# Stick-breaking attention: the causal mask moved from a product on TensorE into the scan on VectorE

## The reference

```
def sb_attend(q, k, v, q_pos, k_pos):
    z = jnp.einsum('bqhd,bkhd->bhqk', q, k) * SB_DIM ** -0.5
    mask = k_pos[None, :] < q_pos[:, None]
    log_1mb = jnp.where(mask, jax.nn.log_sigmoid(-z), 0.0)
    after = lax.cumsum(log_1mb, axis=3, reverse=True) - log_1mb
    att = jnp.where(mask, jnp.exp(jax.nn.log_sigmoid(z) + after), 0.0)
    return jnp.einsum('bhqk,bkhd->bqhd', att, v)
```

## Time and profile before

| what | value |
|---|---|
| median of 3 runs | 1905.25 us (1903.93 to 1905.9) |
| profiled execution | 1906.05 us |
| its span | 1904.5 us |
| TensorE busy | 1778.7 us, 93% |
| VectorE busy | 1054.4 us, 55% |
| ScalarE busy | 866.0 us, 45% |
| GpSimd busy | 121.9 us, 6% |
| the 68 scans, mean | 1423 ns |

### The profile page before, as it was taken

The page is one execution under the profiler, slowest core; times in us unless marked ns, Lnnn a source line. Parts: engine busy times, 40 slices in busy tenths (PEclk is TensorE's granted clock), DMA queues, the critical chain, the costliest instruction groups (busy, mean ns, idle before and its releaser), DMA issues. The chain is left out here.

```text
span 1904.5 us, 25559 instructions
## 1 busy us (share of the span) xinstructions
PE 1778.7 (93%) x10344; PEld 1564.6 (82%) x10344; DVE 1054.4 (55%) x1291; ACT 866.0 (45%) x1112; POOL 121.9 (6%) x136
## 2 busy tenths in 40 slices
PE   7999999899999999999999999969999999999960
PEld 5887777788898879999999998848888888888850
DVE  4326555333245432133243155568888889889857
ACT  4224554323263331121122223247878878878832
POOL 0013000000000021000000000000010000010003
PEclk9999999899999999999999999979999999999985
DMA  5231110202012226111112142169999999999947
GB/s 177 84 103 39 29 29 1 58 23 71 23 42 78 73 60 209 39 45 51 42 42 94 29 172 89 50 248 367 418 415 416 412 415 415 412 413 418 406 149 271
DMA packets 139179, 329.86 MB, mean 173 GB/s; under 512 B 13659, under 2 KB 91319, under 8 KB 114358
## 3 DMA queue, kind: packets, MB, share of 16 engines
q1 hardware_dynamic: 123556, 272.69, 38.7%
q0 software_dynamic: 10896, 38.74, 5.6%
q10 hardware_dynamic: 4608, 16.78, 2.2%
HBM read 286.08 MB, written 39.87 MB: 171 GB/s over the span
## 5 line engine op out<-in xcount | busy, mean ns | idle before, releaser
L2362 DVE TENSOR_TENSOR low<-raw,hig 128x2048 fp32r<-128x2048 f32 x192 | 431.6, 2285 | 68.2 <-ACT hig L2131 67.6
L2131 ACT ACTIVATE hig<-raw 128x2048 fp32r<-128x2048 f32 x192 | 359.4, 1915 | 23.1 <-ACT ye L2202 14.5
L1984 PE MATMUL bank<-hig,xel 128*128 128x512 f32 x512 | 204.3, 399 | 3.9 <-DVE xel L2429 3.9
L1986 PE MATMUL bank<-hig,xeh 128*128 128x512 f32 x512 | 201.1, 393 | 0.0
L1985 PE MATMUL bank<-low,xeh 128*128 128x512 f32 x512 | 200.8, 392 | 0.0
L71 PE MATMUL bank<-xhi,glo 128*128 128x384 f32 (+1 forms) x552 | 180.1, 326 | 3.6 <-ACT sg L2084 2.2
L73 PE MATMUL bank<-xhi,ghi 128*128 128x384 f32 (+1 forms) x552 | 180.0, 326 | 0.0
L72 PE MATMUL bank<-xlo,ghi 128*128 128x384 f32 (+1 forms) x552 | 179.9, 326 | 0.0
L71 PE MATMUL gproj<-xhi,glo 128*128 128x384 f32 (+1 forms) x408 | 142.4, 349 | 3.0 <-DVE glo L1350 3.0
L72 PE MATMUL gproj<-xlo,ghi 128*128 128x384 f32 (+1 forms) x408 | 137.3, 337 | 0.0
L73 PE MATMUL gproj<-xhi,ghi 128*128 128x384 f32 (+1 forms) x408 | 137.0, 336 | 0.0
(11 more groups left out here) (408 smaller groups left out, 3505.6 us busy)
## 6 DMA issues: line engine op xcount, KB each, us to landing
raw<-in_w_e_gate_dram SPq DMA_DIRECT2D x64, 1024.0 KB, 7.8
raw<-in_w_e_up_dram SPq DMA_DIRECT2D x64, 1024.0 KB, 8.2
raw<-in_w_e_down_dram SPq DMA_DIRECT2D x64, 1024.0 KB, 7.5
graw<-in_w_in_dram SPq DMA_DIRECT2D x40, 512.0 KB, 3.8
expert_rows<-ye ACTq DMA_DIRECT2D x32, 512.0 KB, 8.0
xt<-in_x_prompt_dram SPq DMA_DIRECT2D x16, 512.0 KB, 3.7
expert_rows<-nil POOLq DMA_DIRECT2D x16, 512.0 KB, 10.3
braw<-in_w_branch_dram SPq DMA_DIRECT2D x24, 256.0 KB, 2.8
```

Of the source, the lines that this page charges most:

```text
L1984: nc.tensor.matmul(bank[:, :], xel[n % 2][:, kk, :], wh[:, k, :], start=(kk == 0), stop=False)
L1986: last = nc.tensor.matmul(bank[:, :], xeh[n % 2][:, kk, :], wh[:, k, :], start=False, stop=(kk == KC - 1))
L2131: nc.scalar.activation(hig[q % HI][:, :], raw[q % RAW][:, :], ACT.Copy).then_inc(high, 1)
L2362: nc.vector.tensor_tensor(low[q % RAW][:, :], raw[q % RAW][:, :], hig[q % HI][:, :].bitcast(F32), ALU.subtract).then_inc(lowed, 1)
```

## The change

The 64 mask products of the rounds 0 to 7 are gone, and with them the tile `never` and the VectorE instruction that made it. The last score product of each head signals `scored` itself. The "d" rounds keep their mask and their scan. For the others the scan takes a second input, a bf16 table `over` of 960 columns of 0 followed by 128 columns with 1 where the key is hidden, cut to the round's length and read from the right like `sfx`, and its second operation is a maximum. Since running products are at most 1, a 1 in the table holds the product at 1, and a 0 leaves it as it is. GpSimd builds the table ahead of the first cache difference, VectorE waits for it once, before the first scan of round t = 1, and `attT` moves by 1 KB to make room.

```
-    attT = [at("attT", [P, 512], F32, SUF0 + 9216 + 2048 * i) for i in range(3)]
-    assert SUF0 + 15360 <= END
+    attT = [at("attT", [P, 512], F32, SUF0 + 10240 + 2048 * i) for i in range(3)]
+    over = at("over", [P, T - DEC], BF16, SUF0 + 8192)
+    assert SUF0 + 16384 <= R2 + 49152
...
-    never = at("never", [P, P], BF16, CON + 2560)
...
             nc.gpsimd.memset(cvsh[0:1, 0, :], 0.0)
             pool.drain()
+            nc.gpsimd.memset(over[:, 0:T - DEC - P], 0.0)
+            pool.drain()
+            nc.gpsimd.affine_select(out=over[:, T - DEC - P:T - DEC], in_=ones[:, :], compare_op=ALU.is_ge, fill=0.0,
+                                    base=0, pattern=[[1, P]], channel_multiplier=-1)
+            pool.drain()
+            pool.sem_inc(overlaid, 1)
             cache_differ(0)
...
-                            nc.tensor.matmul(zz[u][:, o:o + w], q, k, start=(i == 0), stop=(i == 2 and not diag),
-                                             skip_group_check=True)
+                            product = nc.tensor.matmul(zz[u][:, o:o + w], q, k, start=(i == 0),
+                                                       stop=(i == 2 and not (end and x == "d")), skip_group_check=True)
+                            if x != "d" and end and i == 2:
+                                product.then_inc(scored, 1)
                     k0 += w
-                o, w = sp2[-1]
-                d0 = o + w - (DEC if x == "d" else P)
-                for u in range(len(unit[t])):
-                    nc.tensor.matmul(zz[u][:, d0:o + w], identb[:, :], neverd[:, :] if x == "d" else never[:, :],
+                if x == "d":
+                    o, w = sp2[-1]
+                    nc.tensor.matmul(zz[0][:, o + w - DEC:o + w], identb[:, :], neverd[:, :],
                                      start=False, stop=True, skip_group_check=True).then_inc(scored, 1)
...
-                nc.vector.tensor_tensor_scan(v, v, v, 1.0, ALU.mult, ALU.bypass).then_inc(scanned, 1)
+                if rounds[owner[n]][1] == "d":
+                    nc.vector.tensor_tensor_scan(v, v, v, 1.0, ALU.mult, ALU.bypass).then_inc(scanned, 1)
+                else:
+                    if owner[n] == 1:
+                        ve.wait_ge(overlaid, 1)
+                    cover = over[:, T - DEC - keys[n]:T - DEC][:, ::-1]
+                    nc.vector.tensor_tensor_scan(v, v, cover, 1.0, ALU.mult, ALU.max).then_inc(scanned, 1)
...
-            nc.vector.tensor_scalar(never[:, :], below[:, :], -1.0, 1e30, ALU.add, ALU.mult)
```

More of the change, by code:

```diff
@@ L214, in build @@
             ctx, "q", "wq_in ck_in cv_in qwh qwl qprod ckturned pahigh palow glrd qbuilt")
-        scored, sdone, scanned, tfilled, tcopied, used, ocopied = sems(
-            ctx, "sb", "scored sdone scanned tfilled tcopied used ocopied")
+        scored, sdone, scanned, tfilled, tcopied, used, ocopied, overlaid = sems(
+            ctx, "sb", "scored sdone scanned tfilled tcopied used ocopied overlaid")
         early_in, late_in, last_in, vcol_in, vdiffed, cvdiffed = sems(
@@ L413, in score @@
                 for c, (o, w) in enumerate(sp2):
-                    diag = c == len(sp2) - 1
+                    end = c == len(sp2) - 1
                     for i in range(3):
```

## The result

| | before | changed |
|---|---|---|
| median, first measurement (6 and 6 runs) | 1904.94 us | 1895.34 us |
| ratio, 95% interval | | 0.994, 0.9926 to 0.9955 |
| median, measured again (17 and 6 runs) | 1907.10 us | 1896.38 us |
| ratio, 95% interval | | 0.9949, 0.993 to 0.9968 |
| span of the profiled execution | 1904.5 us | 1897.0 us, the second time 1892.5 us |

The change saves 9.6 us, in the second measurement 10.7; forecast were 6.4 us, 1898.9, in a range from 1895.8. The single times of the changed kernel lie from 1891.7 to 1903.0 us, those of the kernel before in the second measurement from 1903.6 to 1911.5; the three times shown ahead of the prediction had differed by only 2 us.

A forecast was written before the change was run, and what follows sets the result against it. TensorE was taken to bound the masked rounds. 6.5 us from products, less 0.2 for ScalarE, plus 0.1 for the first rounds, gave 6.4 us saved: 1898.9 us from the median of 1905.25, range 1895.8 to 1902.3.

The forecast's parts named there:

- TensorE is the bound in the rounds: Masked rounds, three and a half of four head pairs: TensorE busy 46.69 of 47.6 us, its time saved shortens the span.
- 0.216 us a round, one change of shape instead of two: Average directly after scores in TensorE's queue: one 0.1 us shape change remains; 30 rounds save 6.5 us.
- costs two: Rival: the direct change from scores to average costs two shape changes; 0.11 us a round, 3.3 us saved, 1902.0; 10%.
- is free: Rival: the direct change from scores to average costs nothing; 9.3 us or so saved, 1896; 6%.
- The contrast in the earlier trace: After four transposes, a same-shape query product follows 0.41 us later, scores of another shape 0.61 (0.59 where nothing waits).
- ScalarE gives 0.06 us back in three rounds: Step from 384 to 640 keys, three head pairs: scores wait for sigmoids, gaining 0.15 instead of 0.22; 0.2 us given back.
- The first rounds, 0.1 us: Rounds t=1 and t=2: scans of 1024 begin 0.15 us earlier, at half clock worth 0.07 to 0.15; 0.1 us gained.
- The scan and the table cost nothing: VectorE's scan with bf16 input and maximum keeps its time; GpSimd builds the table while idle for 5.13 us; 0.
- The rival that ends on the other side: Rival: bf16 stream or true maximum slows the scan; if doubled, 32 us more in all, about 1931; 4%.
- What is won here moves all the rest forward.: Everything after this stage starts behind a barrier, loads too, so the stage's gain moves all later work forward.
- TensorE's clock dips at idle places in later stages can fall differently: Uncertainty in later stages, with three shown runs differing by 2 us: forecast's own range 1897.3 to 1900.7, at 75%.
- The low end of the range, 1895.8: Lower limit of the range holding 8 in 10, which takes in the bounds of the shape change's cost.

## Why the prediction was wrong in size, step by step

- **TensorE is the bound in the rounds.** Right. The head pair came down to 45.90 us, forecast 45.9.
- **0.216 us a round, one change of shape instead of two.** Right: 0.27 us from scores to average, and the kernel with masks of the same shape shows the price of a change by itself. The rivals "costs two" and "is free" fall. The contrast in the earlier trace rows was read too smoothly: 0.41 against 0.59 us is 0.18, not 0.1. Taken over all products of the three full-clock head pairs, a change costs 0.10 to 0.15 us, and the larger figure stands at changes from and to the transposes, which are in both kernels.
- **ScalarE gives 0.06 us back in three rounds.** Right, 0.05.
- **The first rounds, 0.1 us.** Not confirmed. The term rested on one trace. What the first head pair takes varies by 2.3 us in kernels with mask products and by 1.5 us in those without, mostly with the clock. Where TensorE was at 1.2 GHz for 6.8 us of it, it took 51.9 and 52.6 us with mask products and 51.0 and 50.8 without; where for 10.2 us, 54.3 and 53.9 against 52.4 and 52.2. That is a gain of 1.4 us and of 1.8, near the 1.4 that the terms make, but so few traces do not resolve 0.1.
- **The scan and the table cost nothing.** Right, taken together (1906.61 against 1907.10), and the scan by itself: 2280 ns as before. The rival that ends on the other side falls.
- **"What is won here moves all the rest forward."** This is the step that failed. It put what the later stages gain at nothing, and they did not just start earlier: they took 3.1 us less in the mean of four traces, by 6.8 us less time at 1.2 GHz. I had allowed under 2 us either way (1897.3 to 1900.7) for "TensorE's clock dips at idle places in later stages can fall differently", and took the narrow spread of the three times shown for the size of that effect. It is larger: adding 2.6 us of idle time to the kernel before takes 3.7 us off, adding 64 short products to the changed one adds 4.4, of which 1.5 lie in the attention stage. The low end of the range, 1895.8, came from the change of shape alone and left it no room. Why the clock is low for less time there stays open.

What the change does in its own stage is therefore the 6.4 us of the forecast (6.6 in the rounds of the traces). The remaining 3 to 4 us of its gain come from the clock in stages that it does not touch, and another edit may take them back, as the 64 products took some 3 us.

## What to carry to other kernels

Count changes of TensorE's array shape as well as products: a small product whose shape differs from its neighbours' on both sides costs its own time and one change more, here half of its price. A mask that keeps a running product at 1 cost nothing here as the scan's second operation. And where a program has stages in which TensorE idles now and then, a gain of a few microseconds upstream is known only to within the clock's answer downstream: take several traces of both kernels, compare them stage by stage, and read the granted clock of each run beside its time.

## What the runs showed of the hardware

- Start to start, a change between the array shapes 64*128, 128*128, 128*64 and 64*64 took 0.10 to 0.15 us more than the product's columns at full clock; between two 128*128 products without a change it was 0.01 to 0.02.
- A scan of 1024 elements took 2280 ns with one f32 tile and a bypass, and with an f32 and a bf16 tile and a maximum. The first two scans of 1024, beside GpSimd's subtractions, took 5.52 and 6.57 us together in two executions of the same kernel, 4.5 alone.
- VectorE stopped for 0.44 us at fixed instructions (number 269 of before in the order of its trace, 268 with one wait more), whatever the time, and adding or removing one instruction near the start of the program moved the stops.
- The same four products behind the same wait of 1.98 us took 2.85 us in the kernel before and 1.88 in the changed one, at a mean granted clock of 0.82 from there to the stage's end against 1.00.
- 64 products of 2.04 us in all, behind the last average of a stage, made that stage 1.5 us longer and the program 4.4; 2.6 us of added idle time made the kernel before 3.7 us faster (ratio 0.9966 to 0.9988). With 1.3 us it was 4.6 us in the median, with an interval that just reaches 1.
